# The even mixer of a two-block transformer kernel as one projection and one pipeline of two-map units

## What is computed

```python
h = x @ w_in                                   # 1024 -> 1952 columns
qa, ka, va, cq, ckv, kr = split(h)             # 512, 512, 512, 256, 128, 32
# A: differential attention, 4 heads x 2 maps, d = 64, values of width 128
q, k = rope(qa), rope(ka)
p = softmax(q @ k.T * 64 ** -0.5)              # for map 0 and map 1
a = (p[map 0] - lam * p[map 1]) @ va
a = rms_norm(a, subln_g) * (1 - lambda_init)
# B: latent attention, 8 heads, keys of 64 + 32, values of width 64
q = rms_norm(cq, q_norm_g) @ w_uq              # 256 -> 8 * 96
kv = rms_norm(ckv, kv_norm_g) @ w_ukv          # 128 -> 8 * (64 + 64)
p = softmax((q_nope @ k_nope.T + rope(q_rope) @ rope(kr).T) * 96 ** -0.5)
b = p @ v
out = concatenate([a, b]) @ w_o                # 1024 -> 1024
```

## Time and profile before

| | |
|---|---|
| median of three runs | 3677.67 us (3677.63 to 3683.33) |
| profiled execution, its own time | 3685.61 us |
| its span, first to last instruction | 3684.3 us |
| granted TensorE clock, mean | 0.941 of 2.4 GHz |
| TensorE matmul busy | 3347.5 us, 91% |
| VectorE busy | 2258.8 us, 61% |
| ScalarE busy | 1816.6 us, 49% |
| GpSimd busy | 337.4 us, 9% |
| even_proj | 1653.7 to 1741.1 us of the span |
| diff | 1741.1 to about 1850 us |
| mla_proj | to about 1905 us |
| mla_0, mla_1 | to about 1994 us |
| mix2_0 | to 2002.0 us, where out2_0's products begin |

### The profile page before, as it was taken

One profiled execution on the slowest core, in us unless ns is written; L12 is line 12 of the kernel. 1 busy time (PEld: TensorE's weight loads), 2 busy tenths in 40 slices (PEclk: granted clock), 3 DMA queues, 4 the chain that ended last, 5 costly groups with the idle time before them and its releaser, 6 DMA issues.

```text
span 3684.3 us, 42208 instructions
## 1 busy us (share of the span) xinstructions
PE 3347.5 (91%) x16628; PEld 2759.5 (75%) x16629; DVE 2258.8 (61%) x3567; ACT 1816.6 (49%) x2699; POOL 337.4 (9%) x278
## 2 busy tenths in 40 slices
PE   8989999999989999998769699999969878999996
PEld 7788777877788778777437577888858767888774
DVE  5655342436655343432644688888953667989886
ACT  3333342324323332422534377888832637888784
POOL 1101000001001000000000211111100211111110
PEclk9978999999988999999789799999979998999998
DMA  4110222212110222222001489898832327999885
GB/s 151 52 55 1 69 92 90 94 69 70 48 54 1 78 83 92 92 92 83 1 23 38 194 326 361 355 353 356 352 111 92 115 106 287 360 360 364 347 356 198
DMA packets 135162, 591.16 MB, mean 160 GB/s; under 512 B 29360, under 2 KB 35632, under 8 KB 110256
## 3 DMA queue, kind: packets, MB, share of 16 engines
q1 hardware_dynamic: 115664, 570.11, 40.1%
q0 software_dynamic: 19296, 18.30, 2.1%
HBM read 594.60 MB, written 44.04 MB: 173 GB/s over the span
## 4 chain that ended last, share of the span: by engine, by line
PE 77%; DVE 10%; DMA 7%; ACT 4%; issue 2%; SPq 0%; DVEq 0%; POOL 0%; ACTq 0%; POOLq 0%
PE ps L189 63%; DMA mem<-in_w_up 5%; PE ps L1779 3%; PE ps L3229 1%; PE ps L1122 1%; PE ps L1764 1%; DMA mem<-in_w_gate 1%; PE ps L1525 1%; PE ps L1765 1%; PE ps L1766 1%; PE ps L1734 1%; PE ps L536 1%; DVE r L3349 1%; ACT r L3294 1%; DVE r L545 1%
## 5 line engine op out<-in xcount | busy, mean ns | idle before, releaser
L189 PE MATMUL ps<-r,r 128*128 128x512 f32 (+4 forms) x10880 | 2557.7, 394 | 69.7 <-DVE r L2188 23.1
L189 PEld LDWEIGHTS ps<-r,r 128*128 128x128 f32 x10880 | 2020.6, 191 | 538.3 <-issue 65.9
L3349 DVE TENSOR_TENSOR r<-mem,r 128x1024 fp32r<-128x1024 f32 x768 | 902.7, 1221 | 133.9 <-ACT r L3294 128.0
L3294 ACT ACTIVATE r<-mem 128x1024 fp32r<-128x1024 f32 x768 | 788.7, 1061 | 226.2 <-PE ps L189 142.9
L686 ACT ACTIVATE r<-mem 128x512 fp32r<-128x512 f32 (+2 forms) x512 | 334.9, 661 | 917.5 <-PE ps L189 912.1
L721 DVE TENSOR_TENSOR r<-mem,r 128x512 fp32r<-128x512 f32 (+1 forms) x272 | 185.7, 688 | 460.3 <-ACT r L686 459.1
L723 DVE SCALAR_TENSOR_TENSOR r<-mem,r 128x512 fp32r<-128x512 f32 (+2 forms) x240 | 167.8, 715 | 257.6 <-ACT r L686 255.9
L3207 POOL DMA_INDIRECT xa<-mem,memu x64 | 101.5, 1586 | 966.8 <-ACT mem L3319 966.8
L189 PE MATMUL ps<-mem 128*128 128x64 f32 (+5 forms) x752 | 131.2, 333 | 29.5 <-DMA mem<-in_nsa_cmp_w 14.9
L189 PEld LDWEIGHTS ps<-mem 128*128 128x128 f32 x752 | 111.9, 219 | 43.7 <-DMA mem<-in_nsa_cmp_w 15.3
L3147 POOL DMA_INDIRECT mem<-xd,memu x64 | 98.6, 1541 | 86.0 <-PE ps L3229 34.3
(11 more groups left out here) (365 smaller groups left out, 2947.8 us busy)
## 6 DMA issues: line engine op xcount, KB each, us to landing
mem<-in_w_up SPq DMA_DIRECT2D x80, 2048.0 KB, 18.2
mem<-in_w_down SPq DMA_DIRECT2D x80, 2048.0 KB, 8.2
mem<-in_w_gate SPq DMA_DIRECT2D x64, 2048.0 KB, 13.2
mem<-in_w_in SPq DMA_DIRECT2D x10, 2048.0 KB, 7.9
mem<-in_odd_w_qkv SPq DMA_DIRECT2D x6, 2048.0 KB, 8.0
mem<-in_w_o SPq DMA_DIRECT2D x4, 2048.0 KB, 10.5
mem<-in_rel SPq DMA_DIRECT2D x16, 512.0 KB, 3.4
mem<-in_even_w_in SPq DMA_DIRECT2D x3, 2048.0 KB, 8.0
```

Source lines behind the costliest of these rows:

```text
L189: r = e.matmul(out, a, b, start=start and i == 0, stop=stop and i == n - 1, skip_group_check=skip)
L3294: act.e.activation(wh, w, ACT.Copy).then_inc(*self.S["ex_wh"](self.l, e, i))
L3349: dve.e.tensor_tensor(wl, w, wh.bitcast(F32), SUB).then_inc(*self.S["ex_wl"](self.l, e, i))
```

## The change

The seven stages become three: EvenProj, EvenMix and the OutRoute stage as it was.

- **EvenProj** is one Dense stage of eight jobs in 38 pieces. The latent columns (chunk 3) come first. While chunk 0 is multiplied, the latent rows are turned (12 transposes), their squares are summed on ScalarE (L2223 on, in the new file), and the rows are split in high and low parts. Then w_uq (2 jobs of 2 pieces, 384 columns) and w_ukv (2 jobs of 1 piece, 512 columns) are multiplied in the rounded type, three products each, with the norm applied to the weights (gain) and to the result (scaled); then chunks 1 and 2. The rotations run on VectorE beside, for all token tiles at once (ropes). The eight small tables are loaded at the stage's beginning. The weights' order is changed to match.
- **EvenMix** is one pipeline of 32 units of two maps. Units 0 to 15 are the two maps of a head of the differential attention; units 16 to 31 are two heads of the latent attention. In TensorE's order, a unit's scores are followed by the transposes of the unit two before and the values of the unit four before. The keys and queries of later heads are turned in between, from a table (due). GpSimd scales map 1 of units 0 to 15 and adds the maps (L2619 and L2620 of the new file), divides both heads' maps of units 16 to 31 by their sums (L2636), and squares four results (L2630). ScalarE no longer scales a map, and VectorE no longer combines. The latent scores are three products of the rounded type instead of one in plain float32. The latent values are written turned: the values are the stationary operand (64 columns for each head of the pair), the weights the moving one, so that the mixed result needs no turning there. The differential results are turned at units 27 to 30.
- The stage mix2_0 is gone. OutRoute waits for each of the eight 128-row blocks of its input by itself (ready), and its first pieces of weights are prepared at the end of EvenMix.

```diff
--- before.py
+++ after.py
...
+    w = A["even_w_in_2"][0]
+    for c in (3, 0, "mla", 1, 2):
+        if c == "mla":
+            out["mla",] = mla
+        else:
+            out["even", c] = dram_chunk(w, 8, (512 * c, min(512, 1952 - 512 * c)))
...
-    def __init__(self, mode, n, chunk, hi, lo, group, first=True, last=True, acts=None, dves=None, gain=None):
+    def __init__(self, mode, n, chunk, hi, lo, group, first=True, last=True, acts=None, dves=None, gain=None, k=8, at=0,
+                 stride=None):
+        self.k, self.at, self.stride = k, at, stride or n
...
+        self.plan = [(job, kk) for job in self.jobs for kk in range(job.k)]
...
+class EvenProj(Dense):
...
+        jobs = [plain(3, 416, 0, lambda j: M.LC[:, j, :]), plain(0, 512, 1, lambda j: M.QK[:, j, 0:512])]
+        for i in range(2):
+            jobs.append(Job("tok", 384, ("mla",), lambda kk: M.LH[:, kk, :], lambda kk: M.LL[:, kk, :], 2 + i, gain=M.qg,
+                            k=2, at=384 * i, stride=768, **scaled(
+                                0, (lambda j, i=i: M.UQ[:, 2 * i:2 * i + 2, j, :],
+                                    lambda ps: ps.rearrange("p (q n) -> p q n", q=2)))))
+        for i in range(2):
+            jobs.append(Job("tok", 512, ("mla",), lambda kk: M.LH[:, 2, :], lambda kk: M.LL[:, 2, :], 4 + i, gain=M.kg,
+                            k=1, at=1536 + 512 * i, **scaled(
+                                1, (lambda j, i=i: M.KF[:, j, 4 * i:4 * i + 4, 0:64], part(0)),
+                                (lambda j, i=i: M.VB[:, j, 256 * i:256 * i + 256].rearrange("p (h d) -> p h d", h=4),
+                                 part(1)))))
+        jobs += [plain(1, 512, 6, lambda j: M.QK[:, j, 512:1024]), plain(2, 512, 7, lambda j: M.V[:, j, :])]
+        super().__init__(K, name, prev, jobs)
...
+        if i == 23:
+            dve.wait_ge("dn_mm", self.p0 + 21)
+            for g in (2, 3):
+                self.out(dve, g)
+            for p in range(4):
+                x = M.UQ[:, p].rearrange("p t (h d) -> p t h d", h=2)[:, :, :, 64:96]
+                ropes(dve, "ev_v", x, 16, M.r2, M.scratch[:, 384 * p:384 * p + 384], "uq", p)
+        if i == 25:
+            self.out(dve, 1)
+            ropes(dve, "ev_v", M.QK[:, :, 0:512].rearrange("p t (n d) -> p t n d", n=8), 8, K.rope, M.scratch, "q")
...
+class EvenMix(Stage):
...
+        self.due, self.claims = {}, []
+        for h in (1, 2, 3):
+            for i, what in enumerate("kq"):
+                self.due[4 * h - 3 + i] = (what, h)
+        for h in range(8):
+            for i, what in enumerate(("mk", "mq")):
+                self.due[11 + 2 * h + i] = (what, h)
+        for h in range(4):
+            self.due[27 + h] = ("x", h)
...
+    def pe_scores(self, pe, n):
...
+            s = 2 * n + m
+            if s >= 3:
+                pe.wait_ge("at_exp", sid, s - 3)
+            bank = K.bank[s % 3][:, :]
+            if n < 16:
+                q, k = M.heads[g % 2]
+                rows = slice(64 * m, 64 * m + 64)
+                r = pe.e.matmul(bank, q[rows, qs], k[rows, :], start=True, stop=True)
+            else:
+                qh, ql, kh, kl = self.pair(2 * (g - 4) + m)
+                r = mm(pe.e, bank, [(qh[:, qs], kh), (qh[:, qs], kl), (ql[:, qs], kh)])
+            r.then_inc(*S["at_qk"](sid, s))
...
+        for j in range(4):
+            ks = slice(128 * j, 128 * j + 128)
+            if n < 16:
+                r = pe.e.matmul(o[:, c], self.tbuf(n, 0)[0][:, ks], M.V[:, j, 128 * g:128 * g + 128], start=j == 0,
+                                stop=j == 3)
+            else:
+                for m in range(2):
+                    h = 2 * (g - 4) + m
+                    r = pe.e.matmul(o[64 * m:64 * m + 64, c], M.VB[:, j, 64 * h:64 * h + 64],
+                                    self.tbuf(n, m)[0][:, ks], start=j == 0, stop=j == 3, skip_group_check=True)
+        r.then_inc(*S["at_pv"](sid, n))
...
+        for n in range(self.UNITS + 4):
+            if n in self.due:
+                self.pe_turn(pe, self.due[n])
+            if n < self.UNITS:
+                self.pe_scores(pe, n)
+            if 0 <= n - 2 < self.UNITS:
+                self.pe_weights(pe, n - 2)
+            if n >= 4:
+                self.pe_values(pe, n - 4)
...
+            for m in range(2) if n < self.UNITS else ():
+                s, (e, before) = 2 * n + m, self.ebuf(n, m)
+                act.wait_ge("at_max", sid, s)
+                if before is not None and before >= 0:
+                    act.wait_ge("at_turn", sid, before, self.maps(before)[-1])
+                act.e.activation(e, K.bank[s % 3][:, :], ACT.Exp, bias=self.negm(s),
+                                 accum_out=self.sums(s)).then_inc(*S["at_exp"](sid, s))
+            u = n - 2
+            if 0 <= u < self.UNITS:
+                dst, before = self.tbuf(u, 0)
+                act.wait_ge("at_turn", sid, u, 0)
+                if before is not None and before >= 0:
+                    act.wait_ge("at_pv", sid, before)
+                act.e.activation(dst, self.turned(u)[0][0][:, :], ACT.Copy).then_inc(*S["at_ev_a"](sid, u, 0))
...
+    def dve_sums(self, dve, n):
+
+        M, S, sid, v = self.M, self.S, self.name, dve.e
+        dve.wait_ge("at_exp", sid, 2 * n + 1)
+        if n < 16:
+            c = M.c[:, n:n + 1]
+            dve.then("em_v", v.reciprocal(c, self.sums(2 * n + 1)))
+            v.tensor_scalar(c, c, self.sums(2 * n), M.lam[:, 2:3], MUL, MUL).then_inc(*S["em_r"](sid, n))
+        else:
+            r = M.SUM[:, 2 * n:2 * n + 2]
+            v.reciprocal(r, r).then_inc(*S["em_r"](sid, n))
...
+        for n in range(self.UNITS + 5):
+            if n < self.UNITS:
+                self.dve_maximum(dve, 2 * n)
+            if 1 <= n <= self.UNITS:
+                self.dve_sums(dve, n - 1)
+            if n < self.UNITS:
+                self.dve_maximum(dve, 2 * n + 1)
+            if n in self.due:
+                self.dve_turned(dve, self.due[n])
+            u = n - 2
+            if 16 <= u < self.UNITS:
+                dst, before = self.tbuf(u, 1)
+                dve.wait_ge("at_turn", sid, u, 1)
+                if before is not None:
+                    dve.wait_ge("at_pv", sid, before)
+                v.tensor_copy(dst, self.turned(u)[1][0][:, :]).then_inc(*S["at_ev_v"](sid, u, 1))
...
+    def pool(self, pool):
+        M, S, sid = self.M, self.S, self.name
+        pool.wait_end(self.prev)
+        for n in range(16):
+            if n >= 8 and n % 4 == 0:
+                self.pool_square(pool, n // 4 - 2)
+            pool.wait_ge("em_r", sid, n)
+            (e0, _), (e1, _) = self.ebuf(n, 0), self.ebuf(n, 1)
+            pool.then("em_n", pool.e.tensor_scalar(e1, e1, M.c[:, n:n + 1], None, MUL), sid, n)
+            pool.e.tensor_tensor(e0, e0, e1, ADD).then_inc(*S["em_c"](sid, n))
+        for n in range(16, self.UNITS):
+            if n in (16, 19):
+                self.pool_square(pool, n // 3 - 3)
+            self.pool_divide(pool, n)
+
+    def pool_square(self, pool, h):
+        M, S, sid = self.M, self.S, self.name
+        x = M.MIX[:, :, 128 * h:128 * h + 128]
+        pool.wait_ge("em_hi", sid, "raw", h)
+        pool.e.tensor_tensor(M.sq[h].rearrange("p (t d) -> p t d", t=4), x, x, MUL).then_inc(*S["em_q"](sid, h))
+
+    def pool_divide(self, pool, n):
+        pool.wait_ge("em_r", self.name, n)
+        for m in range(2):
+            e = self.ebuf(n, m)[0]
+            pool.e.tensor_scalar(e, e, self.sums(2 * n + m), None, MUL).then_inc(*self.S["em_n"](self.name, n, m))
...
-            hi, lo = K.block(K.HTo), K.block(M.lo)
-            before.follow = add(Dense, "even_proj", [
-                Job("tok", 512 if c < 3 else 416, ("even", c), hi, lo, c,
-                    **copies(lambda j, c=c: M.QKV[:, j, 512 * c:512 * c + 512] if c < 3 else M.LC[:, j, :]))
-                for c in range(4)])
-            add(Diff, "diff", M)
-            add(MlaProj, "mla_proj", M)
-            for hg in range(2):
-                add(Mla, f"mla_{hg}", M, hg)
-            mixed, chunk = lambda t: M.MIX[:, t, :], ("even_o",)
+            before.follow = add(EvenProj, "even_proj", M)
+            mix = add(EvenMix, "even_mix", M)
+            chunk, lo = ("even_o",), M.mixed_lo
         else:
             add(Odd, "odd")
-            mixed, chunk = lambda t: Odd.memory(K)[0][:, t, 0:1024], ("odd_o",)
-        lo = base + 20712
-        if l == 0:
-            add(Turn, "mix2_0", lo, mixed)
-        else:
-            add(ColumnTurn, "mix2_1", lo, mixed, False)
-        R = add(OutRoute, f"out2_{l}", l, chunk, lo)
+            mix, chunk, lo = None, ("odd_o",), base + 20712
+            add(ColumnTurn, "mix2_1", lo, lambda t: Odd.memory(K)[0][:, t, 0:1024], False)
+        R = add(OutRoute, f"out2_{l}", l, chunk, lo, mix)
+        if mix:
+            mix.follow = R
```

761 lines of the change are left out of this document (357 added, 404 removed).

## The result

The changed kernel takes 3579.69 us (median of four, 3566.95 to 3585.32) beside 3677.65 us for the kernel before, timed together with it: ratio 0.973, 95% interval 0.970 to 0.977. Timed again later, it took 3575.92 us beside 3678.11: 0.971 (0.969 to 0.973). It is **98 to 102 us faster**; the forecast was 128, and the time lies 30 us above the forecast of 3550 and inside its range.

The account below looks back on a forecast made before the run. Diff was taken as bound by one unit's round through three engines, mla stages by TensorE. Projection +16.3 and mixer 48 + 64 + 5 = 117 start out2_0 127.7 us earlier: 3550 us from the median 3677.7, range 3532 to 3590.

Parts of the forecast that it names:

- rival 2: Differential units: TensorE idles each round and falls to 1.2 GHz, 40 us more, 3590; chance 0.16.
- Projection, +16.3: EvenProj: added products and transposes cost 16.3 us, with splits and rotations covered and small loads hidden at the start.
- Downstream moves with it: After out2_0: everything, including the experts' weight stream, starts earlier by the same 127.7 us.
- Rival 3: Experts' weight stream: it ends where it did and hides the gain, 3678; chance 0.04.
- Differential units, 16 x 3.0 = 48: Units 0 to 15: TensorE's own work and the round through GpSimd both give 3.0 us a unit, 48 us.
- the round's length: Differential units: path from scores through maximum, factor, scaling and addition 4.4 us; with TensorE's part 6.0 for two units.
- The turn was costed as 0.44 us of TensorE's time: Differential units: a turn of 0.44 us in 11 of 16 units, counted as 0.3 us on average.
- The scaling, 0.61 taken: GpSimd's scaling in differential units: 0.61 us assumed from the cast of 64 rows; high end 2.35.
- My own rule (a unit grows by half of it): Differential units: a scaling of 1.22 us lengthens the round by 0.6 and each unit by 0.3, 5 us in all.
- Latent units, 64: Units 16 to 31: scores 1.41, transposes 0.88, values 1.3, about 3.6 us a unit, plus turns 6.6: 64 us.
- Start and end, 5: Mixer: first unit's wait of some 3 us and the root's table loads, counted as 5 us in all.
- the executions' 8 us: Whole kernel before: profiled execution 3685.6 us, 8 over the median of 3677.7; the gain was subtracted from the median.

Follow-up runs that it names:

- t_div: Changed kernel with turn behind the scores, e_latent's edits, and one of each latent unit's two divisions on VectorE: mixer 124.2 us (changed kernel 134.5).
- e_latent: Changed kernel with the fourth head's square one unit later and one norm in each of units 25 to 28: latent part 70.5 us, was 76.0.
- t_stt: Changed kernel with the turn behind the scores and the combination on VectorE as one operation: units 0 to 15 take 47.3 us, was 58.5.
- e_stt: Changed kernel with only the combination put back on VectorE as one operation: units 0 to 15 take 61.3 us, was 58.5.
- e_mix1: Changed kernel with turn behind scores, combination on VectorE, later fourth-head square and spread norms: 3553.37 us, 0.965 of the kernel before.
- f_best: e_mix1 with the third head's square also moved, behind the division of unit 16: 3553.65 us, 0.965 of the kernel before.

## Why the prediction was right, and where it was off

The time lies inside the range, and most of the mechanism held. But the range's high end, 3590, was priced for the low clock of rival 2, and it was used up by other things: a wait and a pipeline's end that had no price, and 13 us that the traces do not place. That it was wide enough for them is luck.

**Projection, +16.3: right.** It has 101.3 us of products, 102.5 forecast; the mixer starts 102.8 us after the projection, 103.6 forecast. Rotations and splits stayed covered.

**Downstream moves with it: right.** The experts' stream began at 2090.10 before; now

```profile
1971.64 0.33 SPq L351 DMA_DIRECT2D mem<-in_w_gate  x1
```

118.5 us earlier, as out2_0 does (119.2), and what follows out2_0's first product kept its length. Rival 3 is out.

**Differential units, 16 x 3.0 = 48: measured 58.5, the largest miss.** The step that failed is the round's length ("the path is then 4.4 us; with the transposes, the values and a turn it is 6.0 us for two units"), in two terms.
1. *The turn was costed as 0.44 us of TensorE's time.* It is also a wait, for VectorE's reading of the turn before, and the unit's scores are queued behind it. Measured: 6.5 us of the 10.5. I followed what waits for GpSimd and not what TensorE's order puts behind each wait.
2. *The scaling, 0.61 taken, 1.57 measured.* The two bounds, 0.61 and 2.35, held it; I took the end that was the cheaper one, from a cast of half the rows. My own rule (a unit grows by half of it) would have given 7.7 us. Taken away alone it gained nothing in the kernel as it is, and once the turn was away the whole of GpSimd's part was worth 4.7 (52.0 to 47.3). Together they gave 58.5 - 47.3 = 11.2; the miss was 10.5.

With the turn moved, the path that the prediction describes is the one in the chain, at 6.8 us for its 6.0, with 0.96 more in the scaling.

The rule of the Trainium skill, "GPSIMD Engine Reference", section 4.1, that elementwise work belongs on VectorE, is borne out by these runs once the turn is moved (47.3 against 52.0), and reversed before it (61.3 against 58.5). On the numbers its two-input half agrees (1.27 on GpSimd, 0.75 on VectorE) and its one-input half, "roughly line-rate", does not: the same scaling of 128x512 took 1.57 us on GpSimd, 0.71 on ScalarE and 0.49 on VectorE (t_div).

**Latent units, 64: right, by terms that cancel little.** Scores 1.39 (1.41), transposes 0.88 (0.88), values 1.02 (1.3), a turn 0.57 (0.44): 3.87 us a unit, 4.0 forecast. The loads of a unit's value products are busy 0.85 us, which is the low end that the prediction did not go below:

```profile
1844.14 0.85 PEld L2453 LDWEIGHTS ps<-mem 128*64 128x64 f32 x16 [0.17 <-issue]
```

The Trainium skill's "TensorEngine Tiling", section Key Properties, would have had the values near the high end for the drains at the changes of mode; they came out near the low end, and no gap of TensorE appears at them. Its other sentence there says that different tiles can load and multiply in parallel. The gain of the alternation (0.5 us) agrees with that, but the runs do not show that it is the reason.

**Start and end, 5: measured 14.** This is the other term that was mis-sized. The latent part is 76.0 us, of which 16 x 3.87 = 62 are units; the start of the pipeline lies in the 58.5. The stop at the square is 4.9 with its low clock (shown by e_latent). The last unit's scores start 11.8 us before out2_0, 7.9 more than a unit: the pipeline of four units runs empty, and I had counted a start but no such end. Tables and norms are 2 to 3 us more, and first units that run in 3.4 to 3.7 take a microsecond back.

**Rival 2, the clock: a small part.** TensorE ran at the lower clock for some 3.5 us around the fifth unit (scores 2.06 us, not 1.11) and behind the square's stop, not through the stage. In the e_latent run, whose first 30 us were at 0.83, the same 16 units took 3 us more.

**From one execution to the median.** The traced stretch explains 16.7 of the 30 us by which the time missed (17.5 in the mixer, less 0.8 at the projection). The other 13 lie between the stretch's 111.0 us in two profiled executions and the 98 to 102 us of the medians. I took the executions' 8 us for a shift that leaves the stretch alone; part of it may lie in the stretch (diff stood at a clock of 0.78). The changed kernel's stretch is 237.3 us in both of its traces. What no edit touches varies in the traces of the changed kernels: 1645.4 to 1658.9 us ahead of the stretch and 1675.8 to 1682.9 behind it. There is only one trace of the kernel before, so where the 13 us lie stays open.

## What to carry to other kernels

When work moves to another engine, write down for each wait what its engine's order has queued behind it: an instruction that costs 0.44 us of time can hold the scores of its unit for as long as another engine takes to empty its bank. Try a cheap reordering of that queue before moving work off the engine that looks slow, since taking work off GpSimd was invisible or harmful until the turn was moved (the combination on VectorE: +2.8 us alone, -4.7 us behind the turn). And this pipeline of depth four has an end that costs as much as two units.

## What was not expected of the hardware

- GpSimd's one-input scaling with a factor for each row (1.57 us for 128x512) is slower than its addition of two inputs (1.27) and its squaring (1.04).
- GpSimd's operations grew where VectorE worked from SBUF to SBUF at the same moment. In t_div, where VectorE's 0.49 us scaling runs at the start of each, the division took 1.86 us instead of 1.57; in t_stt one square that started beside VectorE's combination took 1.56 instead of 1.05 (in e_stt, e_mix1 and f_best one took 1.53 to 1.56):

```profile
1783.85 1.05 POOL L2628 TENSOR_TENSOR mem<-mem 128x512 f32<-128x512 f32 x1 [79.63 <-ACT mem L2509]
1795.97 1.56 POOL L2628 TENSOR_TENSOR mem<-mem 128x512 f32<-128x512 f32 x1 [11.07 <-ACT mem L2509]
```

  VectorE's combination began at 1795.88 and stayed at its 0.75 us. The Trainium skill's "SBUF — State Buffer", section on SBUF's two separate sides, says that the two engines share one pair of ports, that VectorE needs it when both its inputs lie in SBUF and GpSimd reads from there too, and that the one that starts first holds it for its whole instruction. By that rule the square would wait from 1795.97 until 1796.63; it grew by 0.51 us, which roughly agrees. The first square shown started 0.15 us before the end of a combination and did not grow.
- A latent unit's eight value products with 64 stationary columns, four into each half of the columns, take 1.02 us alternating and 1.52 us one half after the other.
- A small factor on VectorE with two pointer operands (128x1) takes 0.27 us, where a reciprocal of the same size takes 0.15.
